# Gathers that begin after two tiles, with the attention of blocks 2 to 7 and the later projections set among their slots

## The reference

```
h   = rms_norm(x) * (1 + scale_m) + shift_m ;  proj = h @ w_in -> u_ssm, c_q, c_kv, k_rope
y_ssm  = s5_group(u_ssm)                       # scan, gelu, y * sigmoid(y @ w_glu + b_glu)
y_attn = mla_group(c_q, c_kv, k_rope)          # 8 heads, causal softmax, query blocks of 128
y   = concat(rms_norm(y_ssm, out_norm_ssm), rms_norm(y_attn, out_norm_attn)) @ w_out
x   = x + gate_m * y
h2  = rms_norm(x) * (1 + scale_f) + shift_f
q   = (h2 @ w_query) -> (token, 8 heads, 2, 128);  s = q . sub_keys        # 2 x 128 scores
s1, i1 = top_k(s[0], 16); s2, i2 = top_k(s[1], 16); top_s, top_c = top_k(s1 + s2, 16)
idx = i1 * 128 + i2 ;  g = softmax(top_s)
out = x + gate_f * sum_over_8x16( g * gelu(expert_down[idx] . h2) * expert_up[idx] )
```

## Time and profile before

| | us |
|---|---|
| median of 3 runs (3353.74 to 3356.37) | 3355.4 |
| the profiled execution | 3357.39 |
| its span, first to last instruction | 3355.6 |
| phase_e, from 378 to 601 | 223 |
| projection, from 601 to 726 | 125 |
| slots, from the first transposes of PE at 766 to the end | 2590 |

### The profile page before, as it was taken

One profiled execution on the slowest core, in us unless ns is written; L12 is line 12 of the kernel. 1 busy time (PEld: TensorE's weight loads), 2 busy tenths in 40 slices (PEclk: granted clock), 3 DMA queues, 4 the chain that ended last, 5 costly groups with the idle time before them and its releaser, 6 DMA issues.

```text
span 3355.6 us, 38552 instructions
## 1 busy us (share of the span) xinstructions
PE 2457.4 (73%) x13234; PEld 2012.0 (60%) x13234; DVE 2215.4 (66%) x5263; ACT 1959.4 (58%) x3667; POOL 1366.9 (41%) x1166
## 2 busy tenths in 40 slices
PE   5967899967777677777776777667667666766676
PEld 4654567536666566666665666556656565655555
DVE  6873655367887666767676666666666676765444
ACT  3213333226767666666676667666766666666665
POOL 1141600014454444444454444444544454444443
PEclk8989889988887777776767767677776777676666
DMA  6600100239999999999999999999999999999997
GB/s 242 184 13 16 51 1 1 102 145 416 421 421 421 421 420 421 418 421 418 421 415 421 415 421 408 421 420 421 409 421 413 421 411 422 418 421 421 421 421 318
DMA packets 172949, 1143.70 MB, mean 341 GB/s; under 512 B 22384, under 2 KB 23296, under 8 KB 41680
## 3 DMA queue, kind: packets, MB, share of 16 engines
q0 software_dynamic: 148352, 1077.61, 77.4%
q1 hardware_dynamic: 23168, 59.42, 5.0%
q10 hardware_dynamic: 1232, 4.20, 0.3%
HBM read 1131.59 MB, written 8.39 MB: 340 GB/s over the span
## 4 chain that ended last, share of the span: by engine, by line
DMA 43%; DVE 16%; PE 11%; ACT 5%; issue 5%; POOL 1%; POOLq 0%; DVEq 0%; SPq 0%
DMA pair_b<-in_experts_dram,idx_g 24%; DMA pair_a<-in_experts_dram,idx_g 18%; DVE pair_b L1472 5%; DVE pair_a L1472 3%; PE outs L1266 3%; PE outa L1266 2%; PE pgg L1248 2%; ACT pair_b L1348 2%; PE outs L1291 2%; PE outa L1291 2%; ACT pair_a L1348 1%; POOL pair_b L1223 1%; DMA wq<-in_w_query_dram 1%; ACT w L1346 1%; DVE top_i L1408 1%
## 5 line engine op out<-in xcount | busy, mean ns | idle before, releaser
L1223 POOL DMA_INDIRECT pair_b<-in_experts_dram,idx_g x612 | 752.6, 1230 | 788.9 <-PE outs L1266 342.0
L1472 DVE SCALAR_TENSOR_TENSOR pair_b<-pair_b,h 128x1024 f32<-128x1024 f32 x612 | 747.7, 1222 | 473.5 <-DMA pair_b<-in_experts_dram,idx_g 449.0
L1223 POOL DMA_INDIRECT pair_a<-in_experts_dram,idx_g x412 | 493.7, 1198 | 688.4 <-PE outs L1266 247.3
L1348 ACT ACTIVATE pair_b<-pair_b,w 128x1024 f32<-128x1024 f32 x612 | 703.0, 1149 | 19.9
L1472 DVE SCALAR_TENSOR_TENSOR pair_a<-pair_a,h 128x1024 f32<-128x1024 f32 x412 | 503.2, 1222 | 313.2 <-DMA pair_a<-in_experts_dram,idx_g 301.9
L1344 ACT ACTIVATE ga<-a 128x1 f32<-128x1 f32 x1024 | 207.0, 202 | 771.0 <-DVE pair_b L1472 443.0
L1266 PE MATMUL outa<-ident,pair_b 128*128 128x128 f32 x2448 | 479.6, 363 | 207.5 <-ACT pair_b L1348 203.2
L1266 PE MATMUL outs<-ident,pair_b 128*128 128x128 f32 x2448 | 440.8, 343 | 202.3 <-ACT pair_b L1348 195.9
L1266 PEld LDWEIGHTS outa<-ident,pair_b 128*128 128x128 f32 x2448 | 393.0, 189 | 288.0 <-ACT pair_b L1348 282.3
L1266 PEld LDWEIGHTS outs<-ident,pair_b 128*128 128x128 f32 x2448 | 363.2, 177 | 269.6 <-ACT pair_b L1348 261.5
L1348 ACT ACTIVATE pair_a<-pair_a,w 128x1024 f32<-128x1024 f32 x412 | 473.3, 1149 | 13.4
...
## 6 DMA issues: line engine op xcount, KB each, us to landing
...
pair_b<-in_experts_dram,idx_g POOLq DMA_INDIRECT x612
...
```

The costliest lines, as they stand in the source:

```text
L1223: p.indirect_dma_start(pair[n % R], None, A["experts"], bass.IndirectOffsetOnAxis(ap=idx[:, t % (2 * PH), k:k + 1], axis=0)).then_inc(pair ...
L1348: s_.activation(pair[n % R][:, D:], pair[n % R][:, D:], ACT.Copy, scale=w[:, n % NA:n % NA + 1]).then_inc(scaled, 1)
L1472: v.scalar_tensor_tensor(down, down, 1.0, S.h2[:, n // P, :], ALU.mult, ALU.mult, accum_out=a[:, n % NA:n % NA + 1]).then_inc(dotted, 1)
```

## The change

- `phase_e` and `phase_f` become one phase, `phase_ef`. Before the slots only the 16 items of blocks 0 and 1 are attended, and only tiles 0 and 1 are projected (FIRST = 2). Slot 0 is gathered when task 0 is found; slot 1 on after both projections.
- The other 48 items stand at slots 8 to 172: scores at slot `AT[m]` on PE, largest and exponential at the next slot (DVE, ACT), the turn and ACT's copy two slots later, the values two more. Tiles 2 to 7 are projected at slots 192, 202, ... 242, each half for itself.
- The ring has 7 buffers in place of 10, since keys, values and queries stay in memory. All copies of turned probabilities are made by ACT. PE adds the mask as a product with the identity.
- The query weights come twice: for tasks 0 to 15 in pieces of 1 MB for each head, where from the second head on the tasks of tiles 0 and 1 share one set of products of 256 columns; then once more in four parts of 2 MB for the other tiles. The output weights and the row vectors are fetched a second time too.
- ACT copies scores into `staged`, from which DVE searches. Softmax batches are one task (tile 0) or two, not four.
- The squares of `yst` are made and summed in phase_c, which also scales `yst` in place of the output weights. x of tiles 2 to 7 comes one at a time.

In the diff's loops over slots PE does everything listed ahead of `add_up(n)`, ACT everything behind `gelu(n)`, DVE everything behind `dot(n)`.

```diff
+            def square_sums(b):
+                if b == 0:
+                    pe.wait_ge(ones_made, 1)
+                pe.wait_ge(sq_ready, b + 1)
+                for n in range(4):
+                    i = 4 * (b % 2) + n
+                    last = t.matmul(t0[:, i:i + 1], squares[:, b % 2, n * P:(n + 1) * P], ones[:], start=b == 0 and n == 0,
+                                    stop=b >= 6, skip_group_check=True)
+                last.then_inc(sq_summed, 1)
...
+                if b >= 1:
+                    square_sums(b - 1)
+            square_sums(7)
...
+            def square_and_scale(b):
+                k, sl = b // 2, slice((b % 2) * 512, (b % 2 + 1) * 512)
+                act.wait_ge(g_mul, b + 1)
+                if b >= 2:
+                    act.wait_ge(sq_summed, b - 1)
+                s.activation(squares[:, b % 2], S.yst[:, k, sl], ACT.Square).then_inc(sq_ready, 1)
+                act.wait_ge(sq_ready, b + 1)
+                s.activation(S.yst[:, k, sl], S.yst[:, k, sl], ACT.Copy, scale=S.vec[:, V_OS + k:V_OS + k + 1])
...
+def phase_ef(nc, A, S):
+    FIRST, R, NA, PARTS = 2, 7, 16, 6
+    LOWEST = -3.0e38
     SCALE = DQK ** -0.5
...
+    wout_of = [place(nc, "wout_a", [P, KD, D], 88), place(nc, "wout_b", [P, KD, D], 32)]
+    rows_of = [place(nc, "rows_a", [P, 3, D], 120), place(nc, "rows_b", [P, 3, D], 64)]
...
+    pair = [place(nc, f"pair{r}", [P, 2 * D], 80 + 8 * r)[:] for r in range(R)]
+    pex = place(nc, "pex", [P, SEQ], 136)
+    pts = place(nc, "pts", [P, SEQ], 140)
...
+    GROUPS = [(0,), (PH,)] + [(h, PH + h) for h in range(1, PH)] + [(t,) for t in range(2 * PH, TASKS)]
     def asked_at(t):
-        return max(PH * (t - 2), TOPK * (t - PH)) if t >= 2 else -1
-
...
+        if t < 2:
+            return -1
+        if t < PH:
+            return 4 if t == 2 else 15 + 12 * (t - 3)
+        if t < 3 * PH:
+            return 212 + 10 * (t - 16) if t < 18 else 256 + 12 * (t - 18)
+        return 16 * t - 56
+
+    def found_at(t):
+        if t < 2:
+            return 4 if t else -1
+        if PH <= t < 2 * PH:
+            return 80 + 14 * (t - PH)
+        return asked_at(t) + 6
...
+    ASKED = {asked_at(group[0]): q for q, group in enumerate(GROUPS) if asked_at(group[0]) >= 0 and q >= 2}
+    WIDE = lambda q: len(GROUPS[q]) - 1
+    QUERIED = {n + 1 + 2 * WIDE(q): q for n, q in ASKED.items()}
+    SCORED = {n + 3 + WIDE(q): q for n, q in ASKED.items()}
+    FOUND = {found_at(t) + m: (t, m) for t in range(1, TASKS) for m in range(PARTS)}
+    TURNED = {asked_at(PH * i) - 4: i for i in range(2, NT)}
+    BATCHES = [(t, t + 1) for t in range(PH)] + [(t, t + 2) for t in range(PH, TASKS, 2)]
+    WEIGHED = {found_at(end - 1) + PARTS: b for b, (first, end) in enumerate(BATCHES) if b >= 1}
+
+    AT, at = {}, 8.0
+    for m in range(EARLY, len(items)):
+        AT[m] = int(at)
+        at += 0.55 * (items[m][0] + 1) + 0.4
+    AT_SCORES = {n: m for m, n in AT.items()}
+    AT_EXP = {n + 1: m for m, n in AT.items()}
+    AT_TURN = {n + 3: m for m, n in AT.items()}
+    AT_VALUES = {n + 5: m for m, n in AT.items()}
+    LAST = {i: AT[i * H + H - 1] for i in range(FIRST, NT)}
+    AT_NORMAL = {n + 6: i for i, n in LAST.items()}
+    AT_SQUARE = {n + 7: i for i, n in LAST.items()}
+    AT_BACK = {n + 8: i for i, n in LAST.items()}
+
+    PROJECT = {192 + 10 * (i - FIRST): i for i in range(FIRST, NT)}
+
+    ACC = (0, 0, 0, 1, 0, 1, 0, 1)
+    END = {P * (i + 1) + (1 if i < 2 else 8): i for i in range(NT - 1)}
...
+            for h in range(1, PH):
+                sp.wait_ge(q_done, h + 1)
+                for n in range(2):
+                    sp.dma_start(pieces[:, n], wp[2 * h + n]).then_inc(piece_in[n], 16)
+            sp.wait_ge(q_done, PH + 1)
+            sp.wait_ge(spilled, 16 * FIRST)
+            sp.dma_start(x2s[:], out[0]).then_inc(x2s_in, 16)
+            sp.dma_start(x2_b[:], x[FIRST]).then_inc(x_in, 16)
+            sp.wait_ge(fin_ready, 1)
+            sp.dma_start(out[0], h2[:, 0, :]).then_inc(stored, 16)
+            sp.dma_start(x2s[:], out[1]).then_inc(x2s_in, 16)
+            sp.wait_ge(at_done, len(items))
+            sp.dma_start(wout_of[1][:], wo).then_inc(wout_in, 16)
+            sp.wait_ge(pv_done, len(items))
+            sp.wait_ge(rows_in, 16)
+            sp.dma_start(rows_of[1][:], rows_kept).then_inc(rows_in, 16)
+            sp.wait_ge(tr_done, NT)
+            sp.wait_ge(rs_std, 1 + NT)
+            sp.dma_start(wq[0][:], wc[0]).then_inc(wq_in[0], 16)
+            for i in range(FIRST, NT):
+                sp.wait_ge(x2_ready, i + 1)
+                sp.dma_start(out[i], x2_b[:]).then_inc(spilled, 16)
+                if i + 1 < NT:
+                    sp.wait_ge(spilled, 16 * (i + 1))
+                    sp.wait_ge(h2_ready, i + 1)
+                    sp.dma_start(x2_b[:], x[i + 1]).then_inc(x_in, 16)
             sp.wait_ge(b_done, NT)
-            for n in range(3):
-                sp.dma_start(wq[:, PH // 2 - 2 - n], w[n + 1]).then_inc(wq_in[n], 16)
...
+                if n == 1:
+                    hold(pool, b_done, FIRST)
+                if n == 5:
+                    pool.wait_ge(h2_ready, FIRST)
+                    hold(pool, rows_in, 16)
...
+            def at_scores(m):
+                i, h = items[m]
+                if m == 0:
+                    pe.wait_ge(mask_ready, 1)
+                elif m == EARLY:
+                    pe.wait_ge(b_read, FIRST)
+                elif i >= 4:
+                    pe.wait_ge(exp_done, m)
+                elif m >= 2:
+                    pe.wait_ge(exp_done, m - 1)
+                sc = half(pb, m)
+                for b in range(0, (i + 1) * P, 512):
+                    end = min(b + 512, (i + 1) * P)
+                    diagonal = end == (i + 1) * P
+                    if diagonal:
+                        t.matmul(sc[:, i * P:end], S.ident[:], mask[:], start=True, stop=False, skip_group_check=True)
+                    last = t.matmul(sc[:, b:end], S.qt[:, i, h, :], S.kt[:, h, b:end], start=not diagonal, stop=True, skip_group_check=True)
+                last.then_inc(at_done, 1)
+
...
+            def at_turn(m):
+                i, h = items[m]
+                pe.wait_ge(exp_done, m + 1)
+                turns_free()
+                for b in range(i + 1):
+                    last = t.transpose(half(tt, m)[:, b * P:(b + 1) * P], half(pex, m)[:, b * P:(b + 1) * P], S.ident[:])
+                last.then_inc(pt_done, 1)
+                evicted["act"] += 1
+                pts_out[m] = evicted["act"]
...
+            at_values(EARLY - 1)
+            project_ssm(0)
+            at_back(FIRST - 1)
+            project_att(0)
+            project_ssm(1)
+            turn(0)
+            queries(0)
+            project_att(1)
+            scores(0)
+            turn(1)
+            for q in (1, 2):
+                queries(q)
+                scores(q)
             for n in range(SLOTS):
+                if n in AT_SCORES:
+                    at_scores(AT_SCORES[n])
+                if n in AT_BACK:
+                    at_back(AT_BACK[n])
+                if n in AT_TURN:
+                    at_turn(AT_TURN[n])
+                if n in AT_VALUES:
+                    at_values(AT_VALUES[n])
+                if n in PROJECT:
+                    project_ssm(PROJECT[n])
+                if n - 3 in PROJECT:
+                    project_att(PROJECT[n - 3])
...
+            def at_exp(m):
+                i, h = items[m]
+                act.wait_ge(top_ready, m + 1)
+                if i >= 4:
+                    act.wait_ge(pt_done, m)
+                elif m >= 2:
+                    act.wait_ge(pt_done, m - 1)
+                if m == EARLY:
+                    act.wait_ge(x2_ready, FIRST)
+                n = (i + 1) * P
+                s_.activation(half(pex, m)[:, 0:n], half(pb, m)[:, 0:n], ACT.Exp, scale=SCALE, bias=top[:, m:m + 1],
+                              accum_out=rsum[:, m:m + 1]).then_inc(exp_done, 1)
+
+            def at_turned(m):
+                i, h = items[m]
+                act.wait_ge(pt_done, m + 1)
+                if i >= 4:
+                    act.wait_ge(pv_done, m)
+                elif m >= 2:
+                    act.wait_ge(pv_done, m - 1)
+                n = (i + 1) * P
+                s_.activation(half(pts, m)[:, 0:n], half(tt, m)[:, 0:n], ACT.Copy).then_inc(tt_out, 1)
...
+                gelu(n)
+                if n in AT_EXP:
+                    at_exp(AT_EXP[n])
+                if n in AT_BACK:
+                    at_back(AT_BACK[n])
+                if n in AT_TURN:
+                    at_turned(AT_TURN[n])
+                if n in AT_SQUARE:
+                    at_square(AT_SQUARE[n])
+                if n - 3 in PROJECT:
+                    project_ssm(PROJECT[n - 3])
...
+            def at_top(m):
+                i, h = items[m]
+                dve.wait_ge(at_done, m + 1)
```

(2 more changed lines are left out.)

826 lines of the change are left out of this document (413 added, 413 removed).

## The result

The changed kernel takes 3415.93 us (median, 3414.53 to 3416.68) against 3355.89 us for the kernel before, measured on the same chip: 1.0175 times as long, 95% interval 1.0161 to 1.0189. It is slower, by 60 us. I had forecast 3338, faster than before, with a range of 3295 to 3375 for the likeliest case and 3250 to 3440 for all of them. The profiled execution took 3416.02 us with a span of 3414.2.

What follows compares the result with a forecast made beforehand. It took the gather stage as bound by DMA transfers, 2.54 us a slot, and ACT as bounding slots 8 to 173. 504 + 14 + 595 + 2160 + 47 + 10 + 9 = 3339 of span, median about 3338 us, range 3295 to 3375.

Steps and rivals of the forecast that it cites:

- likeliest case: Whole kernel: the forecast itself, about 3338 us with a range of 3295 to 3375; chance 0.38.
- slots begin (start): Before the slots: gather 0 leaves at 466 us, steady slots begin at about 504 us, ends 490 and 525.
- the rest: After slot 173: 2160 us of slots, 47 for moved transfers, 10 for idle spells among projections, 9 for the tail.
- item 2: Slots 8 to 173, attention of blocks 2 to 7: ACT bounds, 515 us of work plus 80 of waits, 595 us.
- bounds of 10 and 175: Slots 8 to 173: lowest and highest total of ACT's waits in us, with 80 taken.
- 25 and 37 at full clock: Slots 8 to 173: ACT's waits in us for its exponentials (25) and its copies of turned probabilities (37).
- rival in which the two wait in turn: Slots 8 to 173: PE and ACT wait for each other, 690 us there, 3433 us in all; chance 0.28.
- bounds of 2 to 12 us: phase_c: ends for the time added by 32 products with a column of ones, put at 9 us.
- gain of 262 us: Start: slots begin at about 504 us, where before the slots' transposes kept going from 765.98 us.
- ACT hardly waits: Slots 8 to 173: loads and waits overlap, so 525 us there and 3268 us in all; chance 0.22.
- The dry ring: Seven gather buffers run out once in a task, losing 1 us in 40: +40, 3378 us; chance 0.12.
- slower cases: Whole kernel: all outcomes slower than before, together 0.35, against faster 0.54 and same 0.11.

Runs made afterwards that it cites:

- run without the switches: Changed kernel with the 48 attention exponentials among the slots replaced by Identity and the mask filled with -30: 3300.41 us, ratio 0.9822.
- gelu through tanh slot by slot: Changed kernel with the slots' gelu written by its tanh formula, DVE making its three small operations for each slot alone: 3360.38 us, ratio 1.0006.
- The spread run: Changed kernel with the projections twelve slots apart from slot 182 (not ten from 192) and more slots between their steps: 3381.25 us, ratio 1.0062.
- form by pairs: Gelu through tanh with DVE's operations made for two slots at a time: 3444.91 us in the changed kernel, 3371.35 us in the kernel before.

## Why the prediction was wrong

The sum of the span was 3339 and came out at 3414.2, 75 us more. Each term against its measurement:

| term | predicted | measured | missed by | of it, by cause |
|---|---|---|---|---|
| slots begin (start) | 504 | 526.1 | +22 | phase_c +13, attention to first gather +7, gather to slots +2 |
| slots 0 to 8 | 14 | 15.1 | +1 | |
| slots 8 to 173 | 595 | 615.9 | +21 | ACT's work +1, ACT's waits +20 |
| the rest | 2226 | 2257.1 | +31 | 30 in slots 173 to 262 |

**The frame held.** The bound, the order of the stages, the price of a plain slot (1933.5 us for the last 761 slots, 2.54 each) and the tail were as read, and so was the point from which it decides: item 2 was worth nothing from 612 us on, and came out at 616. That the start and the projections each lost as much again made it clearly slower. The time came out above the range of 3295 to 3375. The steps that failed are three terms of the sum, all too small: phase_c's products priced by their own duration, ACT's waits at 80 us, and 10 us for idle transfers among the projections. The forecast stood only 17 us below the point of no gain.

**The table loads were right.** I counted 123 in the stretch, and there are 123; I put ACT's work at 515 us, and it was 516.1. That each load costs about its own duration and no more was shown by the run without the switches: 1.24 us each. The Trainium skill (ScalarE: Activation LUTs, "Rules for kernel authors") budgets 2.7 us for each switch to another set; by that figure, an estimate, 93 loads would have given back some 250 us, and the trace had 115. The measurement decides: the figure is too high for this place. But the advice of the Trainium skill there, to group by set, names the dearest item of the change: at 1.24 us each the 123 loads are 153 us, more than the 60 by which the kernel is slower. The section "Table sets: the hidden batching unit" of the same page of the Trainium skill lists tanh in the set of exp, and the trace agrees: with gelu through tanh slot by slot ACT loaded a table 5 times ahead of it from 545 to 1000 us, at the five square roots, and never for an exponential of a head.

**ACT's waits were the first mis-sized term.** I took 80 us between bounds of 10 and 175; it was 100, of which 73.8 for PE's turns. I had priced the wait of the copy at 1.8 to 2.3 against 1.6 us a head and full clock, some 37 us in all. The working names both things that make it longer, "more where PE has scores in the same slot" and "at half clock more", but the 80 us are no more than its 25 and 37 at full clock and its 20 behind wide queries: beyond what it took to overlap, the half clock was put at nothing. It judged by the mean clock of a stretch, 0.83, and the mean was right; but around the turns the clock was mostly lower. The copy waited 1.5 us on average (73.8 / 48), and 66.4 of the 73.8 us stand at 33 copies with a granted clock under 0.75. The exponentials, for which I had 25 us, waited 8.2. The run with the copy one slot later shows that the order let these waits in: 47 us for no work removed, though the clock around the turns was hardly higher there (under 0.75 for 35 copies, which waited 3.1 us in all). My rival in which the two wait in turn named the mechanism but not its size: 690 us for the stretch.

**The projections were the second.** I reckoned with sums: 157 us of PE in 215 us of transfers, and gave 10 us for idle spells. But each projection is a chain through PE, DVE, ACT and back, 32.7 us long, in an interval of 25.4. That the slots can't run ahead past it because there are only seven buffers is argued, not shown. The first halves also took 7.5 to 8.6 us instead of 6.87, at a granted clock of 0.84 in the stretch. The spread run took the stretch to 275.3 us, 8 under my own 283: the sum of transfers and work was about right, and the order of steps decides how far above it one lands.

**phase_c was the third.** I asked what 32 products cost (7.6 us + 1.5) and not where they stand. The bounds of 2 to 12 us both lay below the measured 21.8. The step that failed is the one that the working doesn't name: that a moved step costs its own duration and brings no wait. PE now asks for squares that ACT makes only behind PE's own next block. So PE waited 9.2 us and ran three blocks partly at 1.2 GHz for 5.1 more. Asked for one block later the products cost 6.0 us, within the bounds. Of the other +9 at the start, a half projection took 9.70 instead of 6.87 us and a wide pair of queries 10.00 instead of 7.1 (the chain that ended last), at granted clocks of 0.72 and 0.71; the start's upper end of 525 us had been set for such a clock. The rest is spread over many small steps, and I don't break it down further. The terms that the working lists between the first gather and the slots add to 35 us, not to the 38 that it takes; 39.6 were measured. Its gain of 262 us sets PE's transposes of later slots (766) against slot 0 (504); for the scaling of slot 0 in both kernels 504 would have been a gain of 244, and 221.7 were measured. And the DMA share before is 9 tenths from the tenth slice on, not from the fifteenth.

**The rivals.** ACT hardly waits: no. The dry ring: no, the ring of seven costs the kernel before 6 us, and the changed kernel's slots from 262 on are within 5 us of the kernel before (a DMA share of 1.01 and 2.54 us a slot). The sign was that of the slower cases, to which I gave 0.35, and the time, 3416, lies between the forecast and the waiting in turn (3433). It got there without the long stretch of that case: more than two thirds of the miss came from the start and the projections, for which no rival stood.

**What stays open.** Why the tanh form costs 17 us where the transfers set the time (413 instead of 418 GB/s from 2107 to 3095 us) isn't shown; that a buffer comes free later because each slot's chain is longer is argued only. It fits that the form by pairs cost slots 395 to 1023 of the kernel before, with ten buffers, 6.5 us, and those of the changed kernel, with seven, 23.6. Nor is it shown how much of the waits for the turns the lower clock causes, and how much of the lower clock the waits: both went down together in the run without the switches.
